# A chunked RWKV scan whose TensorE and ScalarE orders are rearranged

## What is computed

```python
def step(state, inp):
    r_t, w_t, k_t, v_t, kk_t, a_t = inp
    sa = jnp.einsum('bhvk,bhk->bhv', state, -kk_t)
    state = (state * w_t[:, :, None, :]
             + sa[..., None] * (kk_t * a_t)[:, :, None, :]
             + v_t[..., None] * k_t[:, :, None, :])
    y = jnp.einsum('bhvk,bhk->bhv', state, r_t)
    return state, y
```

## Time and profile before

| | |
|---|---|
| Median of three runs | 2013.53 us |
| The profiled execution, own time | 2015.64 us |
| Its span in the profile | 2013.7 us |
| TensorE matmul busy | 1702.9 us, 85% |
| VectorE busy | 1066.8 us, 53% |
| ScalarE busy | 726.9 us, 36% |
| GpSimd busy | 293.2 us, 15% |
| DMA | 162.96 MB, 81 GB/s on average |
| Mean granted TensorE clock | 0.903 of full speed |

### The profile page before, as it was taken

One profiled execution on the slowest core, in us unless ns is written; L12 is line 12 of the kernel. 1 busy time (PEld: TensorE's weight loads), 2 busy tenths in 40 slices (PEclk: granted clock), 3 DMA queues, 4 the chain that ended last, 5 costly groups with the idle time before them and its releaser, 6 DMA issues.

```text
span 2013.7 us, 27787 instructions
## 1 busy us (share of the span) xinstructions
PE 1702.9 (85%) x11192; PEld 1259.4 (63%) x11192; DVE 1066.8 (53%) x1533; ACT 726.9 (36%) x1159; POOL 293.2 (15%) x124
## 2 busy tenths in 40 slices
PE   0897874888888899999989978568877989999997
PEld 0584432666655688887857834256655768888785
DVE  7254458777533776763333244677772254544333
ACT  1434233455442323232233343445545143232322
POOL 1242000000002122121223400000000222121120
PEclk9999895787788999999999989677788989999999
DMA  6254020000023345452213310000000312222222
GB/s 272 85 177 158 14 84 15 2 2 2 2 105 125 125 173 202 177 198 84 86 62 103 95 64 1 0 2 2 1 2 13 114 54 92 99 88 103 85 85 82
DMA packets 34651, 162.96 MB, mean 81 GB/s; under 512 B 3840, under 2 KB 4096, under 8 KB 25856
## 3 DMA queue, kind: packets, MB, share of 16 engines
q1 hardware_dynamic: 34560, 161.65, 22.7%
HBM read 159.54 MB, written 2.10 MB: 80 GB/s over the span
## 4 chain that ended last, share of the span: by engine, by line
PE 71%; DVE 14%; ACT 7%; issue 6%; DMA 1%; POOL 0%; DVEq 0%; SPq 0%; ACTq 0%; POOLq 0%
PE bank L483 12%; PE bank L485 12%; PE bank L484 12%; PE bank_pair L483 4%; PE bank_pair L485 4%; PE bank_pair L484 4%; DVE work L1316 2%; PE bank L769 2%; PE bank L770 1%; PE bank_pair L573 1%; PE bank L544 1%; PE bank L552 1%; PE bank L747 1%; PE bank L699 1%; PE bank L505 1%
## 5 line engine op out<-in xcount | busy, mean ns | idle before, releaser
L483 PE MATMUL bank<-work_parts,y_mix_parts 128*128 128x512 f32 x792 | 316.2, 399 | 24.1 <-DVE work_parts L1479 15.9
L485 PE MATMUL bank<-work_parts 128*128 128x512 f32 x792 | 314.9, 398 | 0.0
L1492 DVE TENSOR_TENSOR work_parts<-work,y_mix_parts 128x1024 fp32r<-128x1024 f32 x66 | 169.4, 2567 | 254.0 <-ACT y_mix_parts L869 253.9
L1695 POOL TENSOR_TENSOR proj_weights_parts<-proj_weights,proj_weights_hi 128x1024 fp32r<-128x1024 f32 x54 | 132.7, 2460 | 1072.0 <-ACT proj_weights_hi L863 996.2
L1700 POOL TENSOR_TENSOR work_parts<-work,y_mix_parts 128x1024 fp32r<-128x1024 f32 x66 | 160.3, 2429 | 616.1 <-ACT y_mix_parts L869 616.1
L869 ACT ACTIVATE y_mix_parts<-work 128x1024 fp32r<-128x1024 f32 x132 | 132.8, 1054 | 251.8 <-DMA work<-mlp_dram 251.8
L484 PE MATMUL bank<-work_parts,y_mix_parts 128*128 128x512 f32 x528 | 209.0, 396 | 0.0
L483 PEld LDWEIGHTS bank<-work_parts,y_mix_parts 128*128 128x128 f32 x792 | 150.2, 190 | 66.1 <-issue 24.7
L485 PEld LDWEIGHTS bank<-work_parts 128*128 128x128 f32 x792 | 150.3, 190 | 35.6
L483 PE MATMUL bank<-work_parts,proj_weights_hi 128*128 128x512 f32 x304 | 126.9, 417 | 27.0 <-DVE work_parts L1479 12.1
L485 PE MATMUL bank<-work_parts,proj_weights_parts 128*128 128x512 f32 x304 | 124.3, 409 | 0.0
(11 more groups left out here) (252 smaller groups left out, 3185.4 us busy)
## 6 DMA issues: line engine op xcount, KB each, us to landing
work<-mlp_dram SPq DMA_DIRECT2D x66, 1024.0 KB, 4.9
work<-ada_dram SPq DMA_DIRECT2D x64, 512.0 KB, 4.7
proj_weights<-tiles_dram SPq DMA_DIRECT2D x57, 512.0 KB, 3.6
x_res<-ada_dram SPq DMA_DIRECT2D x24, 512.0 KB, 4.9
mixer_inputs<-ada_dram SPq DMA_DIRECT2D x8, 512.0 KB, 15.2
x_res<-x_dram SPq DMA_DIRECT2D x2, 2048.0 KB, 13.7
work<-mlaw_dram SPq DMA_DIRECT2D x4, 640.0 KB, 4.4
out_dram<-x_res SPq DMA_DIRECT2D x8, 256.0 KB, 2.2
```

Source lines behind the costliest of these rows:

```text
L483: mm(out, w_hi, x_hi, start=start, stop=False)
L485: return mm(out, w_lo, x_hi, start=False, stop=stop)
L1492: TTT(MW_L[q][:, 1], MW_IN[q][:, 1], plain(MW_H[q][:, 1]), ALU.subtract).then_inc(msp_v.sem, msp_v.one("l1"))
L1695: pool.tensor_tensor(ring_l[s], ring[s], plain(ring_h[s]), ALU.subtract).then_inc(spl_q.sem, spl_q.one(f"t{s}"))
```

## The change

The order of the scan's steps changes on TensorE and ScalarE, and the right side moves to another bank.

- TensorE: the Gram pair is computed two chunks ahead and stands behind the solve; the value product of the next chunk stands behind it; then the update; then the transposes, also two chunks ahead. Triangle, bonus and tail products now follow all of these. Gram 1 and the transposes of chunk 1 are issued before step 0.
- ScalarE: the eviction of the next chunk's transposes stands in front of the solve's eviction.
- The right side lies in columns 256 to 383 of bank 3, one of the Gram pair's two banks, instead of bank 0. The Gram eviction for chunk s waits for the eviction of R of chunk s - 1.

```diff
+        RHS_P = PS[3][:, 256:384]
...
-        sc_p = steps("sc_p", ["G0", "K0", "L0"] + [n for s in range(NCH) for n in ([f"R{s}"] if s else [])
-                     + ([f"G{s + 1}"] if s < NCH - 1 else []) + [f"SA{s}"]
-                     + ([f"K{s + 1}", f"S{s}", f"L{s + 1}"] if s < NCH - 1 else [])] + ["Y"])
-        sc_a = steps("sc_a", ["T0"] + [n for s in range(NCH) for n in [f"R{s}", f"SA{s}"] + ([f"T{s + 1}"] if s < NCH - 1 else [])])
+        sc_p = steps("sc_p", ["G0", "K0", "G1", "L0", "K1"] + [n for s in range(NCH) for n in ([f"R{s}"] if s else []) + [f"SA{s}"]
+                     + ([f"G{s + 2}"] if s < NCH - 2 else []) + ([f"L{s + 1}", f"S{s}"] if s < NCH - 1 else [])
+                     + ([f"K{s + 2}"] if s < NCH - 2 else [])] + ["Y"])
+        sc_a = steps("sc_a", ["T0"] + [n for s in range(NCH) for n in [f"R{s}"] + ([f"T{s + 1}"] if s < NCH - 1 else []) + [f"SA{s}"]])
...
                     pe.wait_ge(sc_v.sem, sc_v.before(f"G{NCH - 1}", it))
+                    pe.wait_ge(sc_a.sem, sc_a.before(f"R{NCH - 1}", it))
...
-                    last = mm(corner(PS[0], d, e), GR[s % 2][:, e, d, 0:C], TV[s % 2][:, 1, d, e * C:(e + 1) * C],
-                              start=(d == 0), stop=(s == 0), skip_group_check=True)
+                    last = mm(corner(RHS_P, d, e), GR[s % 2][:, e, d, 0:C], TV[s % 2][:, 1, d, e * C:(e + 1) * C],
+                              start=(s == NCH - 1 and d == 0), stop=(s == 0), skip_group_check=True)
...
                 if scan:
+                    scan_gram(it, 1)
                     scan_values(it, 0)
+                    scan_tokens(it, cur, 1)
                 for s in range(NCH):
                     if scan:
                         if s:
                             scan_state(it, s)
+                        scan_solve(it, s)
+                        if s < NCH - 2:
+                            scan_gram(it, s + 2)
                         if s < NCH - 1:
-                            scan_gram(it, s + 1)
-                        scan_solve(it, s)
-                        if s < NCH - 1:
-                            scan_tokens(it, cur, s + 1)
+                            scan_values(it, s + 1)
+                        last = scan_update(it, s)
+                        if s < NCH - 2:
+                            scan_tokens(it, cur, s + 2)
                     if build and s in (0, 1):
                         rwkv_triangle(new, s)
...
-                    if scan:
-                        last = scan_update(it, s)
-                        if s < NCH - 1:
-                            scan_values(it, s + 1)
...
-                        scan_solve(it, s)
                         if s < NCH - 1:
                             scan_ring(it, s + 1)
+                        scan_solve(it, s)
...
                 dve.wait_ge(sc_p.sem, sc_p.at(f"G{s}", it))
+                if s:
+                    dve.wait_ge(sc_a.sem, sc_a.at(f"R{s - 1}", it))
```

More of the change, by code:

```diff
@@ L609, in scan_state @@
                     rows = slice(64 * e, 64 * e + 64)
-                    last = mm(corner(PS[0], d, e), ZR[it % 2][d][rows, s, 0, :], cur[rows, d, :], start=False, stop=True, skip_group_check=True)
+                    last = mm(corner(RHS_P, d, e), ZR[it % 2][d][rows, s, 0, :], cur[rows, d, :], start=False, stop=True, skip_group_check=True)
                 own(sc_p, last, f"R{s}")
@@ L966, in scan_state @@
                 act.wait_ge(sc_p.sem, sc_p.at(f"R{s}" if s else "L0", it))
-                own(sc_a, F(RHS.rearrange("p d v -> p (d v)"), PS[0][:, 0:P], ACT.Identity), f"R{s}")
+                own(sc_a, F(RHS.rearrange("p d v -> p (d v)"), RHS_P, ACT.Identity), f"R{s}")
             def scan_solve(it, s):
```

## The result

The changed kernel takes **2033.18 us** (median of 5 runs, 2027.19 to 2034.59) where the kernel before took 2016.44 (2013.17 to 2018.49) in the same session: ratio **1.0082**, 95% interval 1.0063 to 1.0101. On the forecast's scale that is 2013.53 x 1.0082 = 2030.0. It is slower, as was likeliest, but by four times the forecast's +3.9, and outside its range of 2007 to 2025.

A forecast was written before the change was run, and what follows sets the result against it. VectorE's work plus waits bounds build rounds, TensorE's queue the last rounds. Four tailed rounds +7.4, first rounds -0.8 and 0.0, last rounds -2.7 sum to +3.9 us: 2017.4 from 2013.53, range 2007 to 2025.

The forecast's parts named there:

- Which engine bounds what: A build round is VectorE's program plus its waits; a layer's last, scan-only round is TensorE's queue.
- Steps 0 to 2: Build rounds, scanning one block while inverting the next's triangle: VectorE waits 5.3 for 3.0 us, +2.3 per round.
- Rival 1: Build rounds: TensorE at 2.4 GHz when Gram 2 starts, steps 0 to 2 keep their waits; about 2004; chance 0.20.
- Steps 3 to 6: Build rounds: Gram evictions 4 to 6 wait for nothing; with a tail, Gram eviction 7 waits 1.25 us (0.7 before).
- The last rounds: Each layer's scan-only round: slower start and step 3, faster other steps; -1.35 us per layer, -2.7 in both.
- light step: An undisturbed scan step of the last round: 3.57 us instead of 3.92, TensorE deciding.
- the start: Start of the last round: Gram 1, L0 and K1 stand before solve 0, so R1 comes 1.0 us later.
- first rounds: Each layer's first build round, without a tail: remaining waits vanish, -0.8 and 0.0 us for the two layers.
- Rival 2: New stops split TensorE's work; two low-clock steps at 1.2 us in six rounds, +14, about 2031; chance 0.12.
- Rival 3: Solve not released earlier, light steps stay at 3.9 and only the lag is left; +6.6, 2020; chance 0.08.

The follow-up runs named there:

- filler run: Changed kernel, order untouched, with six of eight chunks of triangle 0 computed an extra time in TensorE's stop before Gram pair 2; 2019.77 us, ratio 1.0013.
- second measurement: The changed kernel run again, unchanged, beside 18 executions of the kernel before; 2030.25 us, ratio 1.0071.
- all four products early: Changed kernel with triangle, bonus, centring and gate products between solve and next Gram pair; 2010.04 us, ratio 0.9958; with bank 0 2006.89, 0.9952.
- fastest kernel: Changed kernel with triangle and bonus products between solve and next Gram pair, and the right side in bank 0; 1989.91 us, ratio 0.9868.
- bank edit: Changed kernel with right side back in bank 0, Gram eviction waiting for its own chunk's transposes instead of R's eviction; 2017.95 us, ratio 1.0018.

## Why the prediction was wrong

**Which engine bounds what: right.** VectorE's busy time in a build round is the same in every kernel here (31.7 to 32.0 in the third round), and the round's length follows its waits.

**Steps 0 to 2, +2.3 per round: right in size and mechanism.** In the four tailed rounds Gram eviction 1 to 3 took 10.13 us on average before (10.50, 10.32, 9.91, 9.81) and 12.42 after (12.29, 12.25, 12.85, 12.27): +2.3. The waits that were named: 2.25 before Gram eviction 2 (forecast 2.55), 1.05 at state 0 (0.97), 1.0 for the key product (1.4), and the rest of L1404's 4.2, 0.6, before Gram eviction 3 (0.4). The assumption behind them, a late rise of the clock, is shown by two windows of after over the same 120 products, Gram eviction 1 to 2 in the first and second round of layer 1:

```profile
1342.23:1347.55 5.32, 4.25 (x120) 3.55 (x120) 3.56 (x8) 2.10 (x6) 0.00 (x0) 1.00 0.01 3
1397.13:1404.65 7.52, 6.44 (x120) 5.42 (x120) 3.56 (x8) 2.10 (x6) 0.00 (x0) 0.62 0.01 2
```

Same instructions, 2.2 us apart, by nothing but the clock (1.00, all at 2.4 GHz, and 0.62). Five of the six rounds of this execution had the low one, 6.92 to 7.76; filling the stop brought all six to 5.32 to 5.87, and the kernel down by 0.58%. The Trainium skill (TensorE: Matmul & The Clock Gate, Part 1) says that activity releases the throttled state; the run with the filler agrees (0.83 to 1.00 in that stretch, for 0.53 to 1.00).

**Rival 1, no lag: its condition was met in one round of six, and its price was wrong.** It said that at full clock steps 0 to 2 keep their waits. The first round of layer 1 had full clock, and eviction 1 to 3 is 10.65 there. In the second round of layer 0 of the filler run (0.97) it is 5.33 + 5.32 = 10.65 too. That is 0.5 longer than before's 10.13. In the third round VectorE still waits up to 1.6 for R1's eviction behind the triangle's. The filler run stands at 1.0013; rival 1's 2004 would be 0.995.

**Steps 3 to 6: here it failed.** The forecast priced these steps at full clock and put VectorE's waits between Gram evictions 3 and 6 at nothing. It doesn't mention the bonus product, while it had priced the triangle, moved in the same way. Gram evictions 4 to 6 indeed wait for nothing. But the bonus product went from before S to behind Gram 5, L4, S3, Y3 and K5, the clock falls in or just behind the stop of 1.73 us ahead of these five, and VectorE waits 1.1 for it. Gram eviction 4 to 5 is 7.32, 7.30, 7.41 and 7.30 in the tailed rounds, for 6.11. That is **+1.2 per round, 4.8 us, missing from the sum**.

The late place alone doesn't make this wait; it takes the low clock as well. The first round of layer 1 of the same execution has the same order and a stop of 1.74 us, but keeps the clock at 1.00. VectorE doesn't wait for the bonus product there, and the stretch is 6.11. The filler run, which leaves the bonus product late, has both outcomes in the two tailed rounds of layer 1:

```profile
1414.97:1422.27 7.30, 6.57 (x62) 4.25 (x63) 6.06 (x12) 1.04 (x3) 0.00 (x0) 0.77 0.01 2
1479.29:1485.40 6.11, 5.28 (x66) 3.53 (x66) 5.97 (x12) 1.31 (x4) 0.00 (x0) 1.00 0.01 3
```

In the new order with the bonus late, 28 of the 36 build rounds of six profiles have this step at 0.61 to 0.77 and 6.99 to 8.32 us, and eight have it at 1.00 and 6.11. With the bonus early, all 30 build rounds of five profiles have 6.11 at 0.98 to 1.00; in half of them the low clock comes one step later, at a lower price (4.95 to 5.53 from Gram eviction 5 to 6, for 4.59). The medians go from 2005.62 to 2001.28 (4.3 us, though the intervals of the two ratios still overlap by 0.001). Whether that is because the bonus product comes sooner or because it fills the stop was not separated. In the kernel before, with the bonus in its old place, one round (the first of layer 0) had the low clock in this step and took 7.18 at 0.78. So the term that was put at nothing is a step at the low clock, and the late bonus product is where VectorE met it.

The rest of these steps was right: Gram eviction 7 waits 1.35 (forecast 1.25), and the stretch before it shrank by 0.35 (forecast 0.45).

**The last rounds, -1.35 each: mis-sized.** They changed by +0.1 and -1.1, mean -0.5, together 1.7 us less gain. Even the -1.1 of layer 1 leans on a start that was slow in the kernel before (6.64 us at 0.51 from Gram eviction 1 to 2, for 5.48 at 0.65 in layer 0). Two terms were too small: the light step is 3.70 for the forecast's 3.57, and the start cost 1.6 for 1.0. One light step of after, against the earlier trace rows:

```profile
552.27 0.31 PEld L612 LDWEIGHTS bank_pair<-rstd,work 64*64 64x64 f32 x8 [0.17 <-issue]
...
552.77 0.28 ACT L970 ACTIVATE rstd<-bank_pair 128x128 f32<-128x128 f32 x1 [1.91 <-PE bank_pair L612]
...
553.15 0.69 DVE L1404 TENSOR_TENSOR work<-bank_pair,constants 128x512 f32<-128x512 f32 x1 [1.29 <-ACT rstd L970]
...
553.89 0.52 PEld L575 LDWEIGHTS bank_pair<-work 64*128 64x128 f32 x8 [0.28 <-DVE work L1404]
...
554.54 0.31 PEld L597 LDWEIGHTS bank_pair<-work 128*64 128x64 f32 x8
554.76 0.32 PEld L635 LDWEIGHTS bank<-work 128*64 128x64 f32 x8
...
555.97 0.31 PEld L612 LDWEIGHTS bank_pair<-rstd,work 64*64 64x64 f32 x8 [0.17 <-issue]
```

The Gram eviction starts 0.88 behind R (forecast 0.83), the next Gram pair 0.74 behind that, at 1.62 (1.57); L to S is 0.22. What was short is the rest up to R, 1.21 for 1.11. With bank 0 the step is 3.49, so the shared bank with its wait costs 0.2 of it. The start costs more because the low clock lasts longer than Gram 1, L0 and K1: it rises near 549.5, behind R1, where it rose near 543.7 before, at R1. There is no stop here to blame. From Gram eviction 1 to 2 the windows show TensorE busy throughout at 0.50, in layer 0 of after (first row). With the new order in the last rounds alone it is the same 5.84 in layer 0, and 4.94 in layer 1, where the rise came within it (second row). Why it comes so late is open.

```profile
543.54:549.38 5.84, 5.84 (x64) 4.60 (x62) 0.98 (x2) 1.51 (x5) 0.00 (x0) 0.50 0.01 3
1511.54:1516.48 4.94, 4.94 (x65) 3.97 (x63) 0.98 (x2) 1.53 (x5) 0.00 (x0) 0.68 0.00 0
```

**The sum rebuilt.** Forecast +3.9; the low clock at the late bonus product +4.8; last rounds +1.7; first rounds +0.2 and -1.3 for -0.8 and 0.0, so -0.3: 10.1, against 10.6 measured in the scans (the rest is the spread of the four tailed rounds). Outside the scans' rounds the two profiled executions differ by +1.0 in all, of which +2.2 is the tail at layer 1's end, at the low clock in one and the high in the other:

```profile
1554.64:1569.13 14.49, 8.05 (x39) 2.90 (x39) 3.30 (x7) 9.56 (x17) 0.00 (x0) 0.56 0.03 4
```

The kernel before took 12.32 there at 0.95. The 5 us by which the medians differ more than the profiled pair are not located by any trace here. With the 13.8 us of the second measurement it would be about 2. The other executions of the changed kernel show 0.003 to 0.005 less granted clock than the profiled one; whether that is the cause is not shown.

**Rival 2 (the clock stays low)** was priced at +14 over the forecast, 2031, and given 0.12. The measured 2030.0 is next to it, in part by luck. Its mechanism, stops that take the clock down, is the one that the sum lacked, and its price of 1.2 us for a low step is what the step from Gram eviction 4 to 5 shows, though it had put the wait before the state and R and not before the bonus product. But it counted two such steps in six rounds. The traces show one, in the four tailed rounds and in one first round (6.99, where the kernel before had 7.18), so 5 us and not 14; the rest of the distance is in the last rounds and in what no trace locates. The filler run points the same way. Its scans are 10.6 us shorter than those of after, 8.0 of it from Gram eviction 1 to 2, which is the forecast's own lag, and 2.1 from 4 to 5, where two rounds kept the clock. A low step should have stood in the sum, or at least in the range. **Rival 3** did not occur: the solve is released early and light steps are shorter.

**The triangle and bonus products' place and the bank cost separately.** With the Gram bank, moving triangle and bonus early is worth 1.0071 - 0.9924 = 0.0147; with bank 0 it is 1.0018 - 0.9868 = 0.0150. The bank is worth 0.0053 with the two late and 0.0056 with them early. With all four products early the bank is worth 0.0006 only (0.9958 to 0.9952, each within about 0.002), so for that order the sum of the two is not shown. Part of it is to be seen: its gate product, early, waits for Ln ahead of S5, and its last rounds take 30.20 and 29.84 from Gram eviction 1 to state 6, where the fastest kernel takes 27.01 in both. The bank edit changes two things, the bank and the awaited instruction, and they were not tried apart. The Trainium skill (PSUM — Partial Sum Buffer, PSUM bank collisions raise a hardware error) says that two engines must not access the same 32 partitions of one bank at once; no run here shows that, but it is the reason for the wait, and its price here is 0.5% of the kernel.

## What to carry to other kernels

When a queue is reordered, price every instruction that changes its place, those of other blocks too: here the same move was worked out for the triangle and left out for the bonus product. And price the steps behind a new stop at the low clock too: the late bonus product cost 1.2 us where the clock fell and nothing where it stayed. That was the largest part of the error that the traces locate. Independent products that are ready belong in the stop that the dependent chain leaves, behind the solve and before the instruction that waits: triangle and bonus there made the kernel faster. One that has a wait of its own doesn't: the gate product there held S5 back behind Ln. A small accumulator laid into a bank that another engine evicts makes that eviction wait for the accumulator's own chain.

## What the runs showed of the hardware

A stop of 1.56 us in TensorE's work, before which it had run at 1.2 GHz, left the stretch from Gram eviction 1 to 2 at a mean granted clock of 0.53 to 0.68 in five rounds of one execution. In the sixth it was 1.00, with no difference in the program: there the clock rose just as the stop began. Filling the stop with 1.50 us of unused products took the six to 0.83 to 1.00, and the kernel from 2030.25 to 2019.77 us.

A stop of 1.73 us at 2.4 GHz was followed by the low level in five of the six rounds (0.76 or 0.77 over the next Gram eviction to Gram eviction) and by no fall in the sixth. And the clock can stay low with no stop at all: at the start of layer 0's last round in the changed kernel TensorE was busy from 540 to 548 at 0.50 throughout.

A late eviction is no measure of who is to blame: with the wait for R gone, the same lag stood as 3.4 us before another instruction of VectorE.
